# First memory's keys with high and low parts side by side: a wide and a narrow product per row chunk, one half copied by ScalarE and the other added by VectorE

## The chip, the cores and the metric

The kernel runs on one core of a Trainium2 chip. The metric is the device time of one launch in microseconds (us); lower is better. Engine names are those of the profile: PE is TensorE (PEld its weight loads), DVE is VectorE, ACT is ScalarE, POOL is GpSimd, SP issues the transfers. Each engine runs its own list of instructions in order, and semaphores tie the lists together.

## What is computed

Two transformer blocks over 256 tokens of width 1024, all in float32. The first block is a gated feed-forward, a mix of two attentions (eight latent heads, "mla", and four differential heads, "diff"), a second feed-forward and a gated embedding. The second block has two layers, each with a mixer, an attention over a memory of 256 rows, and a feed-forward. What the change touches are the memory's keys in the first of these layers:

```python
def memory_cross_attention(x, mem_n, w_q, w_k, w_v, w_o):
    q = (x @ w_q).reshape(B, S, XA_HEADS, XA_DH)
    k = (mem_n @ w_k).reshape(B, -1, XA_HEADS, XA_DH)
    v = (mem_n @ w_v).reshape(B, -1, XA_HEADS, XA_DH)
    s = jnp.einsum('bshd,bmhd->bhsm', q, k).astype(jnp.float32) * (XA_DH ** -0.5)
    p = jax.nn.softmax(s, axis=-1).astype(x.dtype)
```

`mem_n @ w_k` depends on inputs alone, so the kernel computes it long before it is used, between the steps of the first block's attentions.

## The kernel before

**Split numbers.** The large products run in a replicated float32 format whose inputs are cut short, so every operand is kept as a high part and a low part (the rest). A product is three: high by high, high by low, low by high, summed in one bank of PSUM (`three`, L1966 to L1972). A weight block is 128 x 1024 numbers. SP fetches it into one of four raw buffers, ACT writes its high part (`w_hi`, L617), DVE its low part (`w_lo`, L1158), and PE uses it. ACT and DVE work four blocks ahead of PE: each engine's `blk()` stands for "PE has come to this block", and starts the conversion of the block four places on.

**The memory.** Its normalised rows, turned so that features lie on partitions, are held as `m_hi` and `m_lo` (each 128 x 8 x 256). For layer 0 there are 16 memory blocks (`mem_blocks(0, ...)`): first eight for the values, then eight for the keys, called key 0 to key 7 here. A key block is one `chunk` of 8 row chunks: for each, three products with 128 x 128 weights and 256 moving columns, all into the first half of a bank. The banks are 6 and 7 in turn (`k_bank`). ACT then copies the 256 columns to `k_mem` (L804) and adds one to the semaphore `mem_evac`. PE starts key n only when the bank's last user has been copied out:

```python
def k_evacs(l, k):
    if l == 0:
        return 4 + (0 if k < 2 else k if k == 6 else k - 2 if k == 7 else k - 1)
```

So keys 2, 3, 4 and 5 wait for `mem_evac` of 5, 6, 7 and 8: four copies of values, and the keys up to n - 2.

**The loop over twelve heads** (four diff, then eight mla) is where the keys stand. `KV_FILL = (0, 1, 2, 3, 4, 9, 11)` names the rounds with a key block: key 0 comes ahead of the loop, keys 1 to 5 in PE's rounds 0 to 4, key 6 in round 9, key 7 in round 11. In its round i the engines do, in this order:

- PE: the key block; the scores of head i + 1 (L2289 for diff, L2296 for mla); the turn of the probabilities of head i - 1 (L2313), which waits for DVE's last step on them; the weighted sum of head i - 2 (L2326, L2334).
- DVE: `softmax_in(i)` (bias and row maximum: L1512, L1515 for diff, L1518, L1519 for mla; for diff heads from 2 on it waits for the turn of head i - 2); `softmax_out(i - 1)` (division: L1527 to L1533 for diff, L1536, L1538 for mla); if i - 2 is a round with a key, `blk()`, that is a `w_lo` of four blocks on; then the low part of an mla head's output (L1176).
- ACT: the exponentials of head i (L819, L824); if i - 1 is a round with a key, its copy (L804) and a `w_hi`; the copy of turned probabilities (L830); the output copy of head i - 2.

The loop starts some 276 us into the run, and the output projection `w_out` follows it at 328.8 us.

Of the kernel before, what the change touches and what calls it, by code (L numbers as in the profile page):

```python
# [9 lines left out]
F32R = mybir.dt.float32r  # L10
I32 = mybir.dt.int32
ALU = mybir.AluOpType
ACT = mybir.ActivationFunctionType
# [3 lines left out]
P = 128  # L17
S = 256
D = 1024
DC = D // P  # L20
# [22 lines left out]
TILES = 8  # L43
# [125 lines left out]
def build(nc, x_d, xT_d, mem_d, pT, prm_d, id_d, cst_d, late_d, row_d, w_d, out):  # L169
    with ExitStack() as ctx:  # L170
        def sb(name, shape, dt=F32):
            return ctx.enter_context(nc.sbuf_tensor(name, shape, dt))
# [4 lines left out]
        PB = [ctx.enter_context(nc.psum_tensor(f"bank{i}", [P, 512], F32)) for i in range(8)]  # L177
# [8 lines left out]

        x_hi = sb("x_hi", [P, DC, S], F32R)
        x_lo = sb("x_lo", [P, DC, S], F32R)
        m_hi = sb("m_hi", [P, DC, S], F32R)
        m_lo = sb("m_lo", [P, DC, S], F32R)  # L190

        h_hi = sb("h_hi", [P, 8, S], F32R)
        h_lo = sb("h_lo", [P, 8, S], F32R)
# [21 lines left out]
        k_mem = [kv_mem[:, 2 * l, :].rearrange("p (c s) -> p c s", s=S) for l in range(2)]  # L215
# [4 lines left out]
        rs_tok = [tokst[:, 16 + 2 * v:18 + 2 * v] for v in range(4)]  # L220
# [23 lines left out]
        def flat(ap):  # L244
            return ap.rearrange("p a b -> p (a b)")
# [27 lines left out]
        dv, at = region(at, 2, 512)  # L273
# [80 lines left out]
        def sems(names):  # L354
            return [sem(n) for n in names.split()]
# [9 lines left out]
        hi_ready, lo_ready, block_done, vec_chain = sems("hi_ready lo_ready block_done vec_chain")  # L365
        res_ready, xh_ready, xl_ready, y_ready, na_ready, nd_ready, xn_ready, xd_ready, over_alpha = sems(
            "res_ready xh_ready xl_ready y_ready na_ready nd_ready xn_ready xd_ready over_alpha")
        proj_sq, var_ready, lat_norm, lat_t, lat_hi, lat_lo, v_up, vup_evac, dv_evac = sems(
            "proj_sq var_ready lat_norm lat_t lat_hi lat_lo v_up vup_evac dv_evac")
        dq_sum, dq_n, dq_t, diff_evac, dk_n, dk_t = sems(  # L370
            "dq_sum dq_n dq_t diff_evac dk_n dk_t")
        f_gu, k_n, kr_n, k_t, k_evac, q_rot, q_t, q_up = sems("f_gu k_n kr_n k_t k_evac q_rot q_t q_up")
        mem_stat, mem_xn, mem_t, mem_g, mem_hi, mem_lo, mem_evac = sems("mem_stat mem_xn mem_t mem_g mem_hi mem_lo mem_evac")
# [60 lines left out]
        KV_FILL = (0, 1, 2, 3, 4, 9, 11)  # L434
        KV_FREE = 16 - len(KV_FILL)
# [34 lines left out]
        def k_bank(l, k):  # L470
            return PB[(4 if l == 1 and k < 2 else 6) + (k + (l == 0 and k >= 6)) % 2]
# [135 lines left out]
        def _(act):  # L607
# [190 lines left out]
            def mem_blocks(l, lo, hi):  # L798
                for m in range(lo, hi):
                    b = nb[0]  # L800
                    kind, k, i = fill(l, m)
                    if kind == "k":
                        done(b)
                        nc.scalar.activation(k_mem[l][:, k, :], k_bank(l, k)[:, 0:S], ACT.Copy).then_inc(mem_evac, 1)  # L804
                    elif i == 3:
                        done(b)
                        for t in range(2):
                            nc.scalar.activation(v_mem[l][:, t, k * HALF:(k + 1) * HALF], v_bank(l, k)[t][:, :], ACT.Copy, scale=1.0 / ALPHA
                                                 ).then_inc(mem_evac, 1)
                    blk()  # L810
# [100 lines left out]
            for k, (a, n) in enumerate(LAT_PARTS):  # L911
                for t in range(2):
                    nc.scalar.activation(lat_n[:, t, a:a + n], PB[4 + t][:, a:a + n], ACT.Copy,
                                         scale=lat_r[:, 2 * k + t:2 * k + t + 1]).then_inc(lat_norm, 1)
# [27 lines left out]
                nc.scalar.activation(flat(dk[:, 2 * j:2 * j + 2, :]), PB[j][:, :], ACT.Copy, scale=col("g_diff_k")).then_inc(diff_evac, 1)  # L942
            done(blk())
            for t in range(2):
                nc.scalar.activation(dv[:, t, :], PB[2 + t][:, :], ACT.Copy, scale=rs_tok[1][:, t:t + 1]).then_inc(dv_evac, 1)
            mem_blocks(0, 0, 2)
            blk()
            done(blk())
# [63 lines left out]
            for n in range(20):  # L1012
                b = FIRST["ab_in"] + n
# [123 lines left out]
        def _(dve):  # L1137
# [28 lines left out]
            def blk():  # L1166
                behind(nb[0])
                nb[0] += 1
                return nb[0] - 1
# [327 lines left out]
            def mem_blocks(lo, hi):  # L1497
                for m in range(lo, hi):
                    blk()
# [115 lines left out]
            for k, (_, n) in enumerate(LAT_PARTS):  # L1615
                ins = of_raw(lat_ss[:, 2 * k:2 * k + 2], rv[:, 500 + 2 * k:502 + 2 * k], n)
# [69 lines left out]
            for t in range(2):  # L1686
                for g in range(2):
                    k = 2 * t + g
# [10 lines left out]
            settle()  # L1699
            link(nc.vector.tensor_tensor(qr, qr, of_heads(rope_cos[0]), ALU.mult))  # L1700
            nc.vector.tensor_tensor(qr, qr, q_sin, ALU.add).then_inc(q_rot, 1)
            mem_blocks(5, KV_FREE)

            for i in range(NH + 3):
                if i < NH:
                    softmax_in(i, HEADS[i])
                if 1 <= i < NH + 1:
                    softmax_out(i - 1, HEADS[i - 1])
                if i - 2 in KV_FILL:
                    blk()  # L1710
                if i >= 3:
                    head_lo(i - 3, HEADS[i - 3])
                if i == 8:
                    dve.wait_ge(do_stat, 1)
                    link(nc.vector.tensor_scalar(rv[:, 0:S], PB[6][:, 0:S], 1.0 / DIFF_V, RMS_EPS, ALU.mult, ALU.add))
                    rsqrt_guess(rows[:, 0:S], rv[:, 0:S])
                if i in (9, 10):
                    link(rsqrt_steps(rows[:, 0:S], rv[:, 0:S], 1))
                if i == 11:
                    rsqrt_steps(rows[:, 0:S], rv[:, 0:S], 1).then_inc(do_rows, 1)  # L1720
                if i == 12:
                    for h in range(DIFF_HEADS):
                        dve.wait_ge(do_bc, h // 2 + 1)
                        nc.vector.scalar_tensor_tensor(d_out[:, h, :], d_out[:, h, :], g_sub_scaled, half(1 - h // 2, h),
                                                       ALU.mult, ALU.mult).then_inc(do_n, 1)
                if i == 13:
                    for h in range(DIFF_HEADS):
                        dve.wait_ge(do_hi, h + 1)
                        low(x_lo[:, 4 + h, :], d_out[:, h, :], x_hi[:, 4 + h, :], do_lo)
# [120 lines left out]
            for h in range(HG_HEADS):  # L1850
# [6 lines left out]
                for n in range(1, NCHUNK - 1):  # L1857
                    settle()
                    ins = nc.vector.scalar_tensor_tensor(state_of(h, n + 1), state_of(h, n),
                                                         decay[:, h * NCHUNK + n:h * NCHUNK + n + 1],  # L1860
                                                         PB[n % 4][:, n // 4 * P:n // 4 * P + P], ALU.mult, ALU.add)
# [96 lines left out]
        def _(pe):  # L1958
# [6 lines left out]
            def arrived(b):  # L1965
                pe.wait_ge(lo_ready, split_of(b))  # L1966
# [7 lines left out]
            def tile(b, n, w=P):  # L1974
                s = slice(n * P, n * P + w)
                return w_hi[:, slot(b), s], w_lo[:, slot(b), s]

            def chunk(b, out, hi, lo, ready=None):

                arrived(b)  # L1980
                for k in range(TILES):
                    if ready:
                        ready(k)
                    ins = three(out, *tile(b, k), hi[:, k, :], lo[:, k, :], start=k == 0, stop=k == TILES - 1)
                ins.then_inc(block_done, 1)
# [153 lines left out]
            def token_ffn(f, b0):  # L2139
# [114 lines left out]
                                False, True, first=y_ready)  # L2254
                nb[0] = b1 + FFN_BLOCKS

            def mem_blocks(l, lo, hi):
                for m in range(lo, hi):
                    b = blk()
                    kind, n, i = fill(l, m)  # L2260
                    if kind == "k":
                        if l == 0 or n >= 2:
                            pe.wait_ge(mem_evac, k_evacs(l, n))
                        if l == 0 and n == 7:
                            pe.wait_ge(s_max, 10)
                        chunk(b, k_bank(l, n)[:, 0:S], m_hi, m_lo)
                        continue
                    if i == 0 and (l or n):
                        pe.wait_ge(mem_evac, 20 if l else 2)
                        if l and n:  # L2270
                            pe.wait_ge(na_ready, 2 * LN[8] + 2)
                            pe.wait_ge(nd_ready, 2 * LN[8] + 2)
                    arrived(b)
                    for k in range(2):
                        for t in range(2):
                            c, q, w = 2 * i + k, slice(t * P, (t + 1) * P), slice(k * HALF, (k + 1) * HALF)
                            ins = three(v_bank(l, n)[t][:, :], m_hi[:, c, q], m_lo[:, c, q], w_hi[:, slot(b), w], w_lo[:, slot(b), w],
                                        start=i == 0 and k == 0, stop=i == 3 and k == 1)
                    ins.then_inc(block_done, 1)
# [132 lines left out]
            for n, (kind, i) in enumerate(IN_ORDER):  # L2412
# [7 lines left out]
                if n == 9:  # L2420
                    pe.wait_ge(lat_norm, 6)
                    for c in range(3):
                        for t in range(2):
                            ins = nc.tensor.transpose(half(4 + c // 2, c)[:, t * P:(t + 1) * P], lat_n[:, t, c * P:(c + 1) * P], ident)
                    ins.then_inc(lat_t, 1)

            b = blk()
# [33 lines left out]
            pe.wait_ge(mem_lo, 4)  # L2461
            mem_blocks(0, 0, 2)

            pe.wait_ge(diff_evac, 4)
            pe.wait_ge(dv_evac, 2)
            for k in range(2):
                b = blk()
                arrived(b)
                for t in range(2):
                    s = slice(t * P, (t + 1) * P)  # L2470
                    for g in range(2):
                        o = slice(4 * QK * g, 4 * QK * (g + 1))
                        ins = three(PB[2 * t + g][:, 0:4 * QK], h_hi[:, k, s], h_lo[:, k, s], w_hi[:, slot(b), o], w_lo[:, slot(b), o],
                                    start=k == 0, stop=k == 1)
# [393 lines left out]
```

## Time and profile before

| what | value |
|---|---|
| time, median of 3 runs | 1265.15 us (1263.97 to 1265.7) |
| the profiled execution's own time | 1267.17 us |
| its span in the trace | 1265.3 us |
| PE busy, share of the span | 1254.2 us, 99% |
| DVE busy, share of the span | 826.5 us, 65% |
| ACT busy, share of the span | 660.9 us, 52% |
| mean granted TensorE clock | 0.997 of full speed |

A busy PE in the table means that some product was in flight. The start of each product is recorded, and the distance from one start to the next tells how fast PE works; the ends overlap. A timeline row gives the start in us, the duration in us (of all that the row merges), engine, line, operation, tiles written and read, shapes and how many; square brackets hold the idle time ahead and who ended it. A single float32 product is recorded as two, so "x4" is two products in those rows.

### The profile page before, as it was taken

To read this page: it belongs to the slowest core of one execution; us is meant where nothing else is said; L and a number is where in the kernel's file an instruction comes from. 1 tells how busy PE (TensorE), PEld (TensorE's weight loads), DVE (VectorE), ACT (ScalarE), POOL (GpSimd) and SP (SyncE) were. 2 spreads that over 40 slices of the span, in tenths; PEclk is the share of its full clock that TensorE was granted. 3 is DMA by queue.
4 is the path that set the end of the run, shared out by engine and by line. 5 is a ranking of instruction groups with operands and counts; after the bars stand their busy time and mean duration, and the time that the engine had idled before them with its cause. 6 is when DMAs were issued, how large, how long until landed. Compare 5 with 4: busy or idle time off the path is not lost.

```text
span 1265.3 us, 16736 instructions
## 1 busy us (share of the span) xinstructions
PE 1254.2 (99%) x6592; PEld 1077.2 (85%) x6592; DVE 826.5 (65%) x1268; ACT 660.9 (52%) x999; POOL 28.8 (2%) x33
## 2 busy tenths in 40 slices
PE   9999999999999999999999999999999999999998
PEld 8888888888888888899999897888888998888886
DVE  6655666878767565667998665755557575755554
ACT  7544546667574444454526655644445654644443
POOL 0000000010000000000000000000001000000000
PEclk9999999999999999999998999999999999999999
DMA  9655555542355555554424543755555442655552
GB/s 348 216 184 183 185 184 195 170 165 84 126 179 187 184 187 194 184 168 150 150 96 140 199 134 116 249 186 184 198 183 167 167 150 85 228 187 193 189 184 65
DMA packets 62572, 218.94 MB, mean 173 GB/s; under 512 B 6688, under 2 KB 10016, under 8 KB 61984
## 3 DMA queue, kind: packets, MB, share of 16 engines
q1 hardware_dynamic: 62352, 217.63, 51.1%
q8 instruction: 52, 0.85, 0.3%
q10 hardware_dynamic: 144, 0.26, 0.1%
q14 instruction: 24, 0.20, 0.0%
HBM read 216.81 MB, written 1.05 MB: 172 GB/s over the span
## 4 chain that ended last, share of the span: by engine, by line
PE 91%; DVE 7%; ACT 1%; issue 0%; DMA 0%; POOL 0%; DVEq 0%; ACTq 0%; POOLq 0%
PE bank L1970 27%; PE bank L1972 26%; PE bank L1971 26%; DVE arena L1794 3%; PE bank L2194 2%; DVE w_lo L1158 1%; PE bank L2341 1%; PE bank L2302 1%; PE bank L1992 1%; PE bank L2313 1%; PE bank L2405 1%; PE bank L2091 0%; PE bank L2058 0%; PE bank L2296 0%; PE bank L2631 0%
## 5 line engine op out<-in xcount | busy, mean ns | idle before, releaser
L1158 DVE TENSOR_TENSOR w_lo<-w_raw,w_hi 128x1024 fp32r<-128x1024 f32 x382 | 466.3, 1225 | 332.2 <-ACT w_hi L617 330.4
L617 ACT ACTIVATE w_hi<-w_raw 128x1024 fp32r<-128x1024 f32 x382 | 403.3, 1059 | 446.6 <-PE bank L1972 427.7
L1970 PE MATMUL bank<-w_hi,x_hi 128*128 128x512 f32 (+2 forms) x912 | 353.8, 388 | 0.4 <-DVE x_lo L1180 0.4
L1972 PE MATMUL bank<-w_hi,x_lo 128*128 128x512 f32 (+2 forms) x912 | 349.6, 383 | 0.0
L1971 PE MATMUL bank<-w_lo,x_hi 128*128 128x512 f32 (+2 forms) x912 | 349.4, 383 | 0.0
L1972 PEld LDWEIGHTS bank<-w_hi,x_lo 128*128 128x128 f32 x912 | 171.4, 188 | 33.2
L1970 PEld LDWEIGHTS bank<-w_hi,x_hi 128*128 128x128 f32 x912 | 171.5, 188 | 32.7 <-DVE x_lo L1180 0.7
L1971 PEld LDWEIGHTS bank<-w_lo,x_hi 128*128 128x128 f32 x912 | 171.5, 188 | 32.1
L1970 PE MATMUL bank<-w_hi,h_hi 128*128 128x512 f32 (+1 forms) x364 | 142.4, 391 | 0.0
L1972 PE MATMUL bank<-w_hi,h_lo 128*128 128x512 f32 (+1 forms) x364 | 141.3, 388 | 0.0
L1971 PE MATMUL bank<-w_lo,h_hi 128*128 128x512 f32 (+1 forms) x364 | 141.2, 388 | 0.0
L1970 PEld LDWEIGHTS bank<-w_hi,h_hi 128*128 128x128 f32 x364 | 68.3, 188 | 14.7 <-DVE h_lo L1176 1.1
L1972 PEld LDWEIGHTS bank<-w_hi,h_lo 128*128 128x128 f32 x364 | 68.3, 188 | 14.0
L1971 PEld LDWEIGHTS bank<-w_lo,h_hi 128*128 128x128 f32 x364 | 68.4, 188 | 13.5
L1970 PE MATMUL bank<-x_hi,w_hi 128*128 128x256 f32 x256 | 74.3, 290 | 1.5 <-DVE arena L1817 0.9
L1971 PE MATMUL bank<-x_lo,w_hi 128*128 128x256 f32 x256 | 72.4, 283 | 0.0
L1972 PE MATMUL bank<-x_hi,w_lo 128*128 128x256 f32 x256 | 72.4, 283 | 0.0
L1970 PEld LDWEIGHTS bank<-x_hi,w_hi 128*128 128x128 f32 x256 | 49.1, 192 | 2.2 <-DVE arena L1817 1.1
L1794 DVE SCALAR_TENSOR_TENSOR arena<-arena,prm 128x256 f32<-128x256 f32 x120 | 50.0, 478 | 0.5
L1971 PEld LDWEIGHTS bank<-x_lo,w_hi 128*128 128x128 f32 x256 | 49.1, 192 | 0.2
L1972 PEld LDWEIGHTS bank<-x_hi,w_lo 128*128 128x128 f32 x256 | 49.1, 192 | 0.0
L1992 PE MATMUL bank<-xs,w_raw 128*128 128x256 f32 x192 | 43.0, 381 | 0.2 <-DVE xs L1758 0.2
(323 smaller groups left out, 1379.2 us busy)
## 6 DMA issues: line engine op xcount, KB each, us to landing
w_raw<-weights_d SPq DMA_DIRECT2D x394, 512.0 KB, 3.3
arena<-weights_d SPq DMA_DIRECT2D x4, 512.0 KB, 5.7
arena<-ln_rows_d SPq DMA_DIRECT2D x2, 1024.0 KB, 5.6
arena<-late_d SPq DMA_DIRECT2D x1, 1056.0 KB, 5.6
xs<-x_d SPq DMA_DIRECT2D x2, 512.0 KB, 7.4
kv_mem<-mem_d SPq DMA_DIRECT2D x1, 1024.0 KB, 9.4
out_d<-xs SPq DMA_DIRECT2D x4, 256.0 KB, 2.3
arena<-xT_d SPq DMA_DIRECT2D x3, 256.0 KB, 6.2
```

What stands on the lines that cost most here:

```text
L617: nc.scalar.activation(w_hi[:, slot(b), :], w_raw[:, b % RAW, :], ACT.Copy).then_inc(hi_ready, 1)
L1158: nc.vector.tensor_tensor(w_lo[:, slot(b), :], w_raw[:, b % RAW, :], w_hi[:, slot(b), :].bitcast(F32), ALU.subtract).then_inc(lo_ready, 1)
L1794: ins = nc.vector.scalar_tensor_tensor(conv[:, c, :], src, w, conv[:, c, :], ALU.mult, ALU.add)
L1970: nc.tensor.matmul(out, wh, xh, start=start, stop=False, skip_group_check=True)
L1971: nc.tensor.matmul(out, wh, xl, start=False, stop=False, skip_group_check=True)
L1972: return nc.tensor.matmul(out, wl, xh, start=False, stop=stop, skip_group_check=True)
L1992: ins = nc.tensor.matmul(out, w_raw[:, b % RAW, k * P:(k + 1) * P], x[:, k, 0, :], start=k == 0, stop=k == TILES - 1)
L2194: ins = nc.tensor.transpose(PB[2 + k][:, at:at + P], hf[:, t, (2 * k + j) * P:(2 * k + j + 1) * P], ident)
L2302: ins = nc.tensor.matmul(half(n % 2, t), xq[:, 2 * h + k, t * P:(t + 1) * P], k_mem[l][:, 2 * h + k, :], start=k == 0, stop=k == 1)
L2313: ins = nc.tensor.transpose(PB[2 + n % 2][:, k * S + t * P:k * S + (t + 1) * P], e_buf(n)[:, 0, t, k * P:(k + 1) * P], ident)
L2341: ins = nc.tensor.matmul(o[:, c * S:(c + 1) * S], v_mem[l][:, k, at:at + P], pt_buf(n)[:, k, :], start=c == 0 and k == 0, stop=k == 1, ski ...
L2405: nc.tensor.matmul(out, ones, ones, start=True, stop=True)
```

## The change

`m_hi` and `m_lo` become two halves of one buffer `m_hl` (128 x 8 x 2 x 256), so that a row chunk's high and low parts lie side by side. For layer 0's keys, a new `key_chunk` takes the place of `chunk`: with the weights' high part, one product over 512 columns (high and low) into a whole bank; with their low part, one product over 256 columns (high) into the bank's first half. ACT copies the second half to `k_mem` and adds one to a new semaphore `key_side`. DVE waits for that, adds the first half (`key_sum`), and now DVE's add gives `mem_evac`. `key_sum(0)` stands ahead of DVE's loop, the others in the rounds with a `blk()`, behind `softmax_out` and ahead of `blk()`. Layer 1's keys are as before. The semaphore `dv_evac` is merged into `diff_evac`.

```diff
-        m_hi = sb("m_hi", [P, DC, S], F32R)
-        m_lo = sb("m_lo", [P, DC, S], F32R)
+        m_hl = sb("m_hl", [P, DC, 2, S], F32R)
+        m_hi, m_lo = m_hl[:, :, 0, :], m_hl[:, :, 1, :]
...
-                    if kind == "k":
+                    if kind == "k" and l == 0:
+                        done(b)
+                        nc.scalar.activation(k_mem[l][:, k, :], k_bank(l, k)[:, S:2 * S], ACT.Copy).then_inc(key_side, 1)
+                    elif kind == "k":
...
+            def key_sum(k):
+
+                dve.wait_ge(key_side, k + 1)
+                keys = k_mem[0][:, k, :]
+                nc.vector.tensor_tensor(keys, k_bank(0, k)[:, 0:S], keys, ALU.add).then_inc(mem_evac, 1)
+
             mem_blocks(5, KV_FREE)
+            key_sum(0)
...
                 if 1 <= i < NH + 1:
                     softmax_out(i - 1, HEADS[i - 1])
                 if i - 2 in KV_FILL:
+                    key_sum(KV_FREE - DC + KV_FILL.index(i - 2))
                     blk()
...
+            def key_chunk(b, bank):
+
+                arrived(b)
+                for k in range(TILES):
+                    wh, wl = tile(b, k)
+                    nc.tensor.matmul(bank[:, :], wh, flat(m_hl[:, k, :, :]), start=k == 0, stop=k == TILES - 1, skip_group_check=True)
+                    ins = nc.tensor.matmul(bank[:, 0:S], wl, m_hl[:, k, 0, :], start=False, stop=k == TILES - 1, skip_group_check=True)
+                ins.then_inc(block_done, 1)
...
-                        chunk(b, k_bank(l, n)[:, 0:S], m_hi, m_lo)
+                        if l:
+                            chunk(b, k_bank(l, n)[:, 0:S], m_hi, m_lo)
+                        else:
+                            key_chunk(b, k_bank(l, n))
...
-            pe.wait_ge(diff_evac, 4)
-            pe.wait_ge(dv_evac, 2)
+            pe.wait_ge(diff_evac, 6)
```

DVE's list in the kernel before, from the end of round 2 (`softmax_out(1)`, then the `w_lo`) into round 3:

```order
L1530 TENSOR_SCALAR kv_mem<-kv_mem,small 128x256 x2
L1533 SCALAR_TENSOR_TENSOR kv_mem<-kv_mem,small 128x256 [waits vec_chain]
L1533 SCALAR_TENSOR_TENSOR kv_mem<-kv_mem,small 128x256
L1158 TENSOR_TENSOR w_lo<-w_raw,w_hi 128x1024 [waits hi_ready]
L1512 ISA kv_mem,small<-bank,arena 128x256 [waits t_ps,bias_in,s_ps]
```

The same place in the changed kernel (the file's lines have moved by three):

```order
L1533 TENSOR_SCALAR kv_mem<-kv_mem,small 128x256 x2
L1536 SCALAR_TENSOR_TENSOR kv_mem<-kv_mem,small 128x256 [waits vec_chain]
L1536 SCALAR_TENSOR_TENSOR kv_mem<-kv_mem,small 128x256
L1709 TENSOR_TENSOR kv_mem<-bank,kv_mem 128x256 [waits key_side]
L1161 TENSOR_TENSOR w_lo<-w_raw,w_hi 128x1024 [waits hi_ready]
L1515 ISA kv_mem,small<-bank,arena 128x256 [waits t_ps,bias_in,s_ps]
```

The add of key 1 stands between the last step on head 1's probabilities and the `w_lo`, and is the second add to give `mem_evac`.

PE's list in the kernel before, from the scores of head 2 (end of round 1) into key 3 (round 2):

```order
L2289 MATMUL bank<-arena 128x256 [waits s_biased]
L2289 MATMUL bank<-arena 128x256 x3
L2313 MATMUL bank<-ident,kv_mem 128x128 [waits s_prob,q_up]
L2313 MATMUL bank<-ident,kv_mem 128x128 x3
L1970 MATMUL bank<-m_hi,w_hi 128x256 [waits lo_ready,mem_evac]
L1971 MATMUL bank<-m_lo,w_hi 128x256
L1972 MATMUL bank<-m_hi,w_lo 128x256
L1970 MATMUL bank<-m_hi,w_hi 128x256
```

The same place in the changed kernel:

```order
L2312 MATMUL bank<-arena 128x256 [waits s_biased]
L2312 MATMUL bank<-arena 128x256 x3
L2336 MATMUL bank<-ident,kv_mem 128x128 [waits s_prob,q_up]
L2336 MATMUL bank<-ident,kv_mem 128x128 x3
L2273 MATMUL bank<-m_hl,w_hi 128x512 [waits lo_ready,mem_evac]
L2274 MATMUL bank<-m_hl,w_lo 128x256
L2273 MATMUL bank<-m_hl,w_hi 128x512
```

Nothing changes place on PE: three rows of a row chunk are now two, and the key block's first product waits for the same count of `mem_evac`, which another engine now gives.

## Rows read from the trace of the kernel before

**Rows 1.** The page: the chain that ended last, share of the span by engine.

```profile
PE 91%; DVE 7%; ACT 1%; issue 0%; DMA 0%; POOL 0%; DVEq 0%; ACTq 0%; POOLq 0%
```

**Rows 2.** Timeline, PE: 512-column products of a value block, 256-column products of key 0.

```profile
267.87 0.39 PE L1970 MATMUL bank<-w_hi,m_hi 128*128 128x512 f32 x1
...
268.55 0.39 PE L1970 MATMUL bank<-w_hi,m_hi 128*128 128x512 f32 x1
...
273.38 0.28 PE L1970 MATMUL bank<-m_hi,w_hi 128*128 128x256 f32 x1
...
275.54 0.28 PE L1970 MATMUL bank<-m_hi,w_hi 128*128 128x256 f32 x1
```

**Rows 3.** Timeline, PE, rounds 1 to 3: turns, scores, first products of keys 3 and 4.

```profile
285.34 0.66 PE L2313 MATMUL bank<-ident,kv_mem 128*128 128x128 f32 x4
285.75 0.36 PE L1970 MATMUL bank<-m_hi,w_hi 128*128 128x256 f32 x1
...
288.79 1.14 PE L2289 MATMUL bank<-arena 64*128 64x256 f32 x8
289.87 0.66 PE L2313 MATMUL bank<-ident,kv_mem 128*128 128x128 f32 x4
291.04 0.47 PE L1970 MATMUL bank<-m_hi,w_hi 128*128 128x256 f32 x1
...
294.10 1.03 PE L2296 MATMUL bank<-arena 96*128 96x256 f32 x4
```

**Rows 4.** Timeline, PE: key 5, the scores of head 5, the turn of head 5.

```profile
296.08 0.47 PE L1970 MATMUL bank<-m_hi,w_hi 128*128 128x256 f32 x1
...
299.14 1.03 PE L2296 MATMUL bank<-arena 96*128 96x256 f32 x4
...
304.52 0.66 PE L2313 MATMUL bank<-ident,kv_mem 128*128 128x128 f32 x4
```

**Rows 5.** Timeline, DVE, rounds 2 to 5: one row at each point where a step begins.

```profile
286.17 0.42 DVE L1512 CUSTOM_DVE_ANT_0 kv_mem<-bank,rlat 128x256 f32<-128x256 f32 x1 [1.40 <-PE bank L2313]
...
289.54 1.22 DVE L1158 TENSOR_TENSOR w_lo<-w_raw,w_hi 128x1024 fp32r<-128x1024 f32 x1
290.70 0.42 DVE L1512 CUSTOM_DVE_ANT_0 kv_mem<-bank,arena 128x256 f32<-128x256 f32 x1
...
294.06 1.22 DVE L1158 TENSOR_TENSOR w_lo<-w_raw,w_hi 128x1024 fp32r<-128x1024 f32 x1
295.20 0.68 DVE L1518 TENSOR_REDUCE small<-bank 128x2 f32<-128x512 f32 x1
...
297.77 1.22 DVE L1158 TENSOR_TENSOR w_lo<-w_raw,w_hi 128x1024 fp32r<-128x1024 f32 x1
300.20 0.69 DVE L1518 TENSOR_REDUCE small<-bank 128x2 f32<-128x512 f32 x1 [1.21 <-PE bank L2296]
...
303.86 0.61 DVE L1538 TENSOR_SCALAR kv_mem<-kv_mem,small 128x256 f32<-128x256 f32 x2
```

**Rows 6.** Timeline, ACT: the copy of key 1.

```profile
285.02 0.36 ACT L804 ACTIVATE kv_mem<-bank 128x256 f32<-128x256 f32 x1
```

**Rows 7.** Timeline, DVE: a 128 x 256 step that reads a bank.

```profile
310.50 0.42 DVE L1715 TENSOR_SCALAR rv<-bank 128x256 f32<-128x256 f32 x1 [0.89 <-PE bank L2347]
```

**Rows 8.** Timeline, PE: the turn of head 11.

```profile
325.06 0.66 PE L2313 MATMUL bank<-ident,kv_mem 128*128 128x128 f32 x4 [1.04 <-DVE kv_mem L1538]
```

**Rows 9.** Busy us by stretch (PE, PEld, DVE, ACT, POOL), then granted clock, DMA.

```profile
670.00:675.00 5.00, 5.00 (x28) 5.00 (x28) 3.91 (x6) 0.66 (x2) 1.53 (x1) 0.57 0.32 104
675.00:680.00 5.00, 5.00 (x35) 5.00 (x34) 4.86 (x16) 2.56 (x7) 0.84 (x2) 0.75 0.33 109
```

**Rows 10.** Timeline, PE, around that stretch.

```profile
669.80 2.76 PE L2637 MATMUL bank<-ones,arena 128*128 128x1 f32 x16
...
675.45 0.41 PE L1970 MATMUL bank<-m_hi,w_hi 128*128 128x256 f32 x1
675.66 0.41 PE L1971 MATMUL bank<-m_lo,w_hi 128*128 128x256 f32 x1
```

More of the change, by code:

```diff
@@ L367, in build @@
             "res_ready xh_ready xl_ready y_ready na_ready nd_ready xn_ready xd_ready over_alpha")
-        proj_sq, var_ready, lat_norm, lat_t, lat_hi, lat_lo, v_up, vup_evac, dv_evac = sems(
-            "proj_sq var_ready lat_norm lat_t lat_hi lat_lo v_up vup_evac dv_evac")
+        proj_sq, var_ready, lat_norm, lat_t, lat_hi, lat_lo, v_up, vup_evac, key_side = sems(
+            "proj_sq var_ready lat_norm lat_t lat_hi lat_lo v_up vup_evac key_side")
         dq_sum, dq_n, dq_t, diff_evac, dk_n, dk_t = sems(
@@ L944, in _ @@
             for t in range(2):
-                nc.scalar.activation(dv[:, t, :], PB[2 + t][:, :], ACT.Copy, scale=rs_tok[1][:, t:t + 1]).then_inc(dv_evac, 1)
+                nc.scalar.activation(dv[:, t, :], PB[2 + t][:, :], ACT.Copy, scale=rs_tok[1][:, t:t + 1]).then_inc(diff_evac, 1)
             mem_blocks(0, 0, 2)
```

## The prediction

> **What bounds the kernel now.** I read the page's chain first: it is PE for 91% of the span [rows 1], and PE is busy 99% of it. What shortens PE's stream shortens the run, and what makes PE wait lengthens it by as much, unless a wait stood there already. The second view is PE's timeline at the two widths that matter. A 512-column product starts every 0.227 us (0.68 over three), a 256-column one every 0.120 us (2.16 over eighteen) [rows 2]: 0.2135 per 512 columns, and some 0.0135 that each product costs beside its columns. The third is the loop over the heads, engine by engine. PE's keys fill the time in which DVE does the softmax: key 3 starts at 285.75, and when it and the scores behind it are through, the turn of head 1 starts at 289.87 [rows 3], 0.3 us after DVE has finished head 1's probabilities at about 289.6 (the `w_lo` behind them starts at 289.54) [rows 5]. So key 3 covers exactly the time that DVE needs. I asked of each key what it waits for now and what it waits for then.
>
> **The products: a small gain.** Before, a row chunk is 3 x 0.120 = 0.360 us; after, 0.227 + 0.120 = 0.347. A block of eight row chunks gets 0.104 shorter, eight blocks 0.83 us. The columns are the same 768; only one product's fixed cost in three goes. The weight loads go from three to two as well, but they run beside the products.
>
> The Trainium skill ("TensorE: Matmul & The Clock Gate", section "Back-to-back issue gap") gives the fixed part of a warm product as about 2.5 ns; by that figure the 64 products saved would be an estimated 0.16 us. The rows show 13 ns at both widths, and the trace decides.
>
> **ScalarE's side** costs nothing: it copies 256 columns per key as before (0.36 us [rows 6]), from the other half of the bank. The high and low parts' new places change no count of instructions, and the merged semaphore waits for the same copies.
>
> **The adds.** DVE gets eight of them, 128 x 256, one input from a bank. The nearest row is a step of that size that reads a bank, 0.42 us [rows 7]. That would be 3.4 us on an engine that is 65% busy. Their place matters more than their length, because the copy that lets PE go on is now the last of three steps on DVE.
>
> **Key 3, the wait that the change adds.** Key 3 waits for `mem_evac` of 6, that is for key 1 to be out of bank 7. Before, ACT's copy of key 1 ends at 285.02 + 0.36 = 285.38 [rows 6], ahead of key 3's start at 285.75: PE did not wait. After, the count comes from `key_sum(1)`, which DVE's list holds in round 2 behind `softmax_in(2)` and `softmax_out(1)`. DVE starts the first at 286.17 and is through the second at 289.54 [rows 5]; the add takes 0.42 and the hand-over to PE 0.05 (the turn at 304.52 against a DVE step that ends at 303.86 + 0.61 = 304.47 [rows 4, 5]). That is 290.0. The add of key 0 ahead of the loop puts off round 0 by up to 0.42, of which PE's earlier end of keys 0 to 2 takes some back; I take 0.2. Key 3 starts at 290.2 where it started at 285.75: **+4.4 us**. Queued behind it on PE are the scores of head 3 and the turn of head 1, and behind these scores stands DVE's next round. Key 3 no longer covers the softmax; it follows it, and the next softmax follows key 3.
>
> **Key 4.** It waits for the add of key 2, in DVE's round 3. From key 3's start: key 3 to the scores behind it 288.79 - 285.75 - 0.10 = 2.94; scores to turn 1.08 [rows 3]; from the turn's start to `softmax_in` 286.17 - 285.34 = 0.83 [rows 3, 5] (a diff head's waits for that turn); `softmax_in(3)` and `softmax_out(2)` 294.06 - 290.70 = 3.36 [rows 5]; add and hand-over 0.47. Sum 8.68, so key 4 starts at 298.9, against 291.04 before [rows 3]: **+7.8 us**.
>
> **Key 5.** It waits for the add of key 3, in DVE's round 4. Key 4 to the scores of head 4: 294.10 - 291.04 - 0.10 = 2.96 [rows 3]; scores to `softmax_in` of an mla head 300.20 - 299.14 = 1.06 [rows 4, 5]; `softmax_in(4)` and `softmax_out(3)` 297.77 - 295.20 = 2.57 [rows 5]; 0.47. Sum 7.06, so 305.9 against 296.08 [rows 4]: **+9.8 us**. That is the end of this chain: key 6 comes in round 9 and key 7 in round 11, and the adds that they wait for are rounds back by then.
>
> **The rest of the loop.** The scores of head 5 follow key 5 at +9.7. The adds of keys 4 and 5 lie in DVE's rounds 5 and 6, where DVE releases PE without slack: the turn of head 5 starts 0.05 after its DVE step [rows 4, 5]. Of their 0.84 I take 0.7. Keys 6 and 7 give back 0.2. The add of key 6 lies in DVE's round 11, in which PE already waits 1.04 us for DVE at 325.06 [rows 8]: +0.4. The add of key 7 falls between other waits and costs between 0 and 0.4; I take 0, since the first two weight blocks' products of the output projection cover the low parts that come behind it. Together 9.7 + 0.7 - 0.2 + 0.4 = **+10.6 us**. After the loop PE is the bound again and nothing gives back a delay that all engines share.
>
> **The clock.** PE is quiet from the end of the turn of head 0 (about 286.0) to 290.2, then from about 295.7 to 298.9 and from about 304.2 to 305.9. The trace has one place where the granted clock fell. It was 0.57 in 670 to 675 and 0.75 in 675 to 680 [rows 9]; with 0.5 (1.2 of 2.4 GHz) as the lower level that is 4.3 + 2.5 = 6.8 us at half. Ahead of it PE had only one-column products and a few transposes [rows 10]. A 256-column product then started every 0.21 us [rows 10]. Such a fall costs at most half of its 6.8 us, 3.4, and less where part of it passes in a quiet stretch. Key 3's block all at half would take 2.8 us more by doubling; the pitch says 0.09 us per 256 columns, 8 x 3 x 0.093 = 2.2. So I take 2.3 for a fall in the quiet ahead of key 3, and 1.2 for the second quiet, three quarters as long, as about even odds of another: **+3.5 us**, with 0 and 10.2 (three full falls) as ends.
>
> The Trainium skill (same page, section "What's actually happening") says that a quiet TensorE is throttled to half its clock and comes back after sustained work; the fall in the trace agrees. What that adds is in the 3.5.
>
> **Sum.** The profiled execution has a span of 1265.3 in a time of 1267.17, and the median is 1265.15; I add the difference to the median. 10.6 + 3.5 = 14.1, which gives **1279.3 us**.
>
> **The rivals.**
>
> *The clock holds.* The chain of waits is as worked out, but no quiet stretch brings a fall: 1265.15 + 10.6 = 1275.8. For it: the quiets are a few us long, with dense products between. Against it: the trace's fall came with PE working, if sparsely.
>
> *The clock falls in every round.* Three falls near the full 3.4: 1275.8 + 10.2 = 1286. It needs each fall to lie wholly in work, while the quiets take a part of each.
>
> *The adds come in time (not slower).* DVE is idle for 1.40 us up to 286.17 [rows 5], and key 1's copy is out at 285.38 [rows 6]; an add in that gap would end near 285.8, and key 3 would not wait. It decides at key 3's old start, 285.75: if the count of 6 is there by then, the keys stay covers, only the 0.83 is left, and the time is 1264.3; with the adds of rounds 5, 6 and 11 charged, 1265.4. Against it: DVE's list holds the add behind `softmax_out(1)`, and engines do not change places in their lists.
>
> *Only part of the chain forms.* If DVE's rounds shrink since they no longer share anything with PE, or keys 4 and 5 find their counts sooner than summed, the delay is key 3's 4.4 and a part of the rest: 1270 to 1273.
>
> **How the numbers follow.** The forecast, chain and one or two falls, gets 0.62; the clock that holds 0.18; falls in every round 0.09; part of the chain 0.06; adds in time 0.05. The range leaves out the last two and the far end of the third: 1274.8 (the clock holds, less 1.0 for the small terms) to 1285. A measurement of this kernel can tell about 0.2%, 2.5 us, from no change. Faster by that much would need 2.5 us where the products give 0.83: 0.01. Within it: 0.05. Slower: 0.94.
>
> **What would show it.** In the profile after: 512-column products of the keys every 0.227 us and narrow ones every 0.120; idle time of some 4 us on PE (or its weight loads) ahead of key 3, 3 ahead of key 4 and 1.7 ahead of key 5, released by DVE's add; key starts near 290.2, 298.9 and 305.9 with a full clock, later by 2 to 3 with a fall; an add of 0.42; the granted clock below 1 between 286 and 312 and nowhere new; the output projection some 14 us later than at 328.8. Wrong would be: no wait of PE on the add; ACT's copy as the last step; a wide product that takes more than two narrow ones; or a delay of the loop that does not show in the end.

## Result, and the profile after

| | before | after |
|---|---|---|
| median | 1265.34 us (4 runs) | 1280.08 us (1278.79 to 1280.41, 4 runs) |
| span of the profiled execution | 1265.3 us | 1278.0 us |
| PE busy | 1254.2 us | 1256.0 us |
| DVE busy | 826.5 us | 829.2 us |
| ACT busy | 660.9 us | 660.5 us |
| mean granted clock | 0.997 | 0.995 |

The changed kernel is slower: the ratio is 1.0111, with a 95% interval of 1.0099 to 1.0123, some 14.7 us. The forecast was 1279.3. One execution of the first variant below, the one with narrow products, took 3036.11 us and is left out of its ratio. The engines' busy times have hardly moved. What has moved is when they work. The waits of PE in the loop over the heads (engine, line, who it waited for: total us, times, longest), in the changed kernel:

```profile
PE bank L2273 <- DVE kv_mem L1709: 8.9, 3, 4.0
PE bank L2336 <- DVE kv_mem L1541: 2.2, 3, 1.5
PE bank L2312 <- DVE small L1515: 0.3, 1, 0.3
```

L2273 is the wide product, L1709 DVE's add: three waits, 8.9 us, which the kernel before does not have. Where they stand, in PE's timeline (start, duration; first product of keys 3, 4 and 5, and what PE does around them):

```profile
286.84 0.66 PE L2336 MATMUL bank<-ident,kv_mem 128*128 128x128 f32 x4
291.51 0.80 PE L2273 MATMUL bank<-m_hl,w_hi 128*128 128x512 f32 x1 [4.01 <-DVE kv_mem L1709]
...
296.64 1.14 PE L2312 MATMUL bank<-arena 64*128 64x256 f32 x8
297.72 0.66 PE L2336 MATMUL bank<-ident,kv_mem 128*128 128x128 f32 x4
298.21 1.03 PE L2349 MATMUL bank<-kv_mem,arena 128*128 128x256 f32 x4
302.38 0.50 PE L2273 MATMUL bank<-m_hl,w_hi 128*128 128x512 f32 x1 [3.15 <-DVE kv_mem L1709]
...
310.95 0.50 PE L2273 MATMUL bank<-m_hl,w_hi 128*128 128x512 f32 x1 [1.79 <-DVE kv_mem L1709]
```

In [rows 3] key 3 starts 0.4 us after the start of the turn ahead of it; here it is 4.7 us. DVE's side of the first wait, and what the wait then does to DVE:

```profile
287.68 0.42 DVE L1515 CUSTOM_DVE_ANT_0 kv_mem<-bank,rlat 128x256 f32<-128x256 f32 x1 [1.34 <-PE bank L2336]
...
291.04 0.42 DVE L1709 TENSOR_TENSOR kv_mem<-bank,kv_mem 128x256 f32<-128x256 f32 x1
291.37 1.22 DVE L1161 TENSOR_TENSOR w_lo<-w_raw,w_hi 128x1024 fp32r<-128x1024 f32 x1
298.55 0.42 DVE L1515 CUSTOM_DVE_ANT_0 kv_mem<-bank,arena 128x256 f32<-128x256 f32 x1 [5.96 <-PE bank L2336]
```

The add ends at 291.46 and PE starts at 291.51. After its `w_lo` DVE is idle for 5.96 us, for PE. In [rows 5] the two softmax rounds follow each other at 286.17 and 290.70, with no idle time. PE waits for DVE, then DVE for PE: what ran side by side now takes turns.

The granted clock (the column after the five engines' busy times), by stretch:

```profile
285.00:290.00 5.00, 2.50 (x18) 1.60 (x16) 3.55 (x17) 3.98 (x14) 0.00 (x0) 0.94 0.01 2
290.00:295.00 5.00, 3.49 (x11) 3.02 (x12) 2.55 (x5) 2.67 (x8) 0.00 (x0) 0.50 0.28 86
295.00:300.00 5.00, 4.24 (x23) 2.98 (x21) 1.45 (x8) 1.25 (x3) 0.00 (x0) 0.87 0.05 19
300.00:305.00 5.00, 2.62 (x10) 2.25 (x11) 3.36 (x11) 3.29 (x10) 0.00 (x0) 0.81 0.11 24
305.00:310.00 5.00, 4.16 (x20) 3.31 (x18) 2.01 (x7) 1.40 (x4) 0.00 (x0) 0.85 0.21 81
```

With 0.5 as the lower level (1.2 of 2.4 GHz), the missing parts are (0.06 + 0.50 + 0.13) x 10 = 6.9 us for the first fall and (0.19 + 0.15) x 10 = 3.4 us for the second. While the clock is at half, the wide products of key 3 start every 0.64 us:

```profile
292.31 0.63 PE L2273 MATMUL bank<-m_hl,w_hi 128*128 128x512 f32 x1
292.75 0.41 PE L2274 MATMUL bank<-m_hl,w_lo 128*128 128x256 f32 x1
292.96 0.63 PE L2273 MATMUL bank<-m_hl,w_hi 128*128 128x512 f32 x1
```

At full clock, in key 0 and key 5, a row chunk takes 0.35.

To set runs side by side I use distances from key 0's first product, since its start differs by up to 1.3 us between executions (272.94 to 274.24):

| us from key 0's start to | key 3 | key 4 | key 5 | key 6 | key 7 | output projection |
|---|---|---|---|---|---|---|
| before | 12.81 | 18.10 | 23.14 | 39.34 | 46.54 | 55.88 |
| after | 17.27 | 28.14 | 36.71 | 53.42 | 60.53 | 70.19 |
| difference | +4.46 | +10.04 | +13.57 | +14.08 | +13.99 | +14.31 |

The loop alone has grown by 14.3 us. The spans differ by 12.7 only; the last experiments show why.

### The profile page after: what moved, and what is told of

Read it like the earlier page. It is cut to its first block, busy times and chain, and to the rows that moved or that the text cites. A ratio compares the mean times of both kernels' runs of the same rounds, so it can differ in the third digit from the quotient of the medians.

```text
span 1278.0 us, 16616 instructions
## 1 busy us (share of the span) xinstructions
PE 1256.0 (98%) x6528; PEld 1073.6 (84%) x6528; DVE 829.2 (65%) x1276; ACT 660.5 (52%) x999; POOL 28.9 (2%) x33
## 4 chain that ended last, share of the span: by engine, by line
PE 87%; DVE 9%; DMA 1%; ACT 1%; issue 1%; SPq 0%; POOL 0%; DVEq 0%; ACTq 0%; POOLq 0%
PE bank L1981 26%; PE bank L1983 25%; PE bank L1982 25%; DVE arena L1805 3%; DVE w_lo L1161 2%; PE bank L2205 2%; DMA w_raw<-weights_d 1%; PE bank L2273 1%; PE bank L2364 1%; PE bank L2325 1%; PE bank L2003 1%; PE bank L2274 1%; PE bank L2336 1%; ACT w_hi L617 0%; PE bank L2069 0%
## 5 line engine op out<-in xcount | busy, mean ns | idle before, releaser
L1981 PEld LDWEIGHTS bank<-w_hi,h_hi 128*128 128x128 f32 x364 | 68.3, 188 | 14.7 <-DVE h_lo L1179 1.1
```

Source lines behind the costliest of these rows:

```text
L1981: nc.tensor.matmul(out, wh, xh, start=start, stop=False, skip_group_check=True)
```

## Experiments

Three theories stood against each other. **The wait**: an add behind `softmax_out` in DVE's list makes the key blocks follow the softmax, and the loss is what stands ahead of the add; the clock falls in the quiets that this makes. **The work**: the eight adds cost as work on DVE, wherever they stand. **The product**: the wide product or the new layout is slow.

### The product: three narrow products, all else as changed

```diff
-                    nc.tensor.matmul(bank[:, :], wh, flat(m_hl[:, k, :, :]), ...)
+                    nc.tensor.matmul(bank[:, 0:S], wh, m_hl[:, k, 0, :], ...)
+                    nc.tensor.matmul(bank[:, S:2 * S], wh, m_hl[:, k, 1, :], ...)
```

> The changed kernel with three narrow products per row chunk (the high by low one into the bank's second half), and the same copy, add and waits. The theory of the wait: the products are a small matter, so nearly the whole 14.7 us stay, and the time is the changed kernel's 1280.1 plus up to 0.8, 1280 to 1281.5; key 3 still starts some 4 us after the turn. The rival, that the wide product or the new layout is what costs: back to 1265 to 1268.

Measured: 1279.28 us against 1266.81 for the kernel before in the same job, ratio 1.0095 (1.0077 to 1.0114). That is 12.5 us more, and the time lies below the expected 1280 to 1281.5; no run looks for the cause, but the fall of the clock behind the loop, with which this section ends, is of about this size. The loop does show the expected size: key 0 to the output projection takes 70.63 us, 14.75 more than before and 0.44 more than with the wide product. PE's waits for the add are the same:

```profile
PE bank L2273 <- DVE kv_mem L1709: 8.9, 3, 4.0
PE bank L2337 <- DVE kv_mem L1541: 2.1, 3, 1.4
```

So the product theory falls: with the old products the loss stays. By the loop of the two traces the wide product is a gain, and a small one; the run times cannot tell it.

### The place of the add: at the head of DVE's round

```diff
             for i in range(NH + 3):
+                if i - 2 in KV_FILL:
+                    key_sum(KV_FREE - DC + KV_FILL.index(i - 2))
                 if i < NH:
...
                 if i - 2 in KV_FILL:
-                    key_sum(KV_FREE - DC + KV_FILL.index(i - 2))
                     blk()
```

> The changed kernel with each add moved to the head of DVE's round, ahead of softmax_in, into the idle time that DVE has there. The theory of the wait: key 3 starts within 0.3 us of the turn before it, the granted clock stays full in the loop, and the time is 1264.3 to 1266.5 (the adds of rounds 3 to 6 may still push the softmax by 0.4 each). The rival, that the eight adds cost as work on DVE wherever they stand: 1268 or more.

Measured: 1267.22 us against 1266.81 us for the kernel before in the same job, ratio 1.0005 (0.9996 to 1.0014): no difference that can be told. The forecast was given on a base of 1265.3; as a difference from the kernel before it was -1.0 to +1.2, and 0.4 was measured. DVE's first add in the loop, and key 3 on PE:

```profile
286.24 0.42 DVE L1709 TENSOR_TENSOR kv_mem<-bank,kv_mem 128x256 f32<-128x256 f32 x1 [0.64 <-ACT kv_mem L804]
286.95 0.42 DVE L1515 CUSTOM_DVE_ANT_0 kv_mem<-bank,rlat 128x256 f32<-128x256 f32 x1 [0.29 <-PE bank L2337]
```

```profile
286.12 0.66 PE L2337 MATMUL bank<-ident,kv_mem 128*128 128x128 f32 x4
286.72 0.50 PE L2274 MATMUL bank<-m_hl,w_hi 128*128 128x512 f32 x1
```

The add fits into idle time that DVE had, and the 8.9 us of waits are gone. Key 3 starts 0.60 us after the turn, where 0.3 was expected and the kernel before has 0.41. The same adds, the same products, the same copies: the place of one line in DVE's list is worth all of the loop's 14.3 us but 1.25. Key 0 to the output projection takes 57.13 us, 1.25 more than before, although the eight key blocks are shorter. A part of that stands ahead of key 2, where PE waits for the row maximum of round 0, and DVE now has the add of key 0 ahead of it:

```profile
280.96 1.14 PE L2313 MATMUL bank<-arena 64*128 64x256 f32 x8 [0.34 <-DVE small L1515]
```

### The place again: between the two halves of the softmax

```diff
                     softmax_in(i, HEADS[i])
+                if i - 2 in KV_FILL:
+                    key_sum(KV_FREE - DC + KV_FILL.index(i - 2))
                 if 1 <= i < NH + 1:
                     softmax_out(i - 1, HEADS[i - 1])
                 if i - 2 in KV_FILL:
-                    key_sum(KV_FREE - DC + KV_FILL.index(i - 2))
                     blk()
```

> The changed kernel with each add between softmax_in and softmax_out of its round. The theory of the wait, by the same rows: key 3 +2.6, key 4 +4.2, key 5 +4.4 and the loop +5.3 against the kernel before; the quiets are 2.2 and 1.5 us, so no fall or one of 2: ratio 1.004 to 1.0055, that is 5 to 7 us. The rival, a loss that does not grow with what stands ahead of the add on VectorE: as at the head of the round (same as before) or as behind softmax_out (14 us).

Measured: 1273.54 us against 1266.17, ratio 1.0060 (1.0047 to 1.0073), 7.4 us. PE's waits are at keys 3 and 4, and key 5 finds its count:

```profile
289.16 0.50 PE L2274 MATMUL bank<-m_hl,w_hi 128*128 128x512 f32 x1 [2.23 <-DVE kv_mem L1709]
297.67 0.50 PE L2274 MATMUL bank<-m_hl,w_hi 128*128 128x512 f32 x1 [1.36 <-DVE kv_mem L1709]
```

```profile
290.00:295.00 5.00, 5.00 (x24) 3.87 (x23) 2.02 (x3) 2.12 (x6) 0.00 (x0) 0.66 0.32 105
```

Key 3 is at 15.50 us from key 0, +2.7 against the kernel before (expected 2.6). The granted clock of 0.66 in one stretch is 3.4 us at half. Key 3's products take 4.35 us from the first start to the last, where the run with filler below, at full clock, has 2.81, so the fall costs 1.5. The loop takes 62.73 us, +6.85, and less 1.5 that is +5.3, as expected. The time is a little above the expected 5 to 7 us; the interval (6.0 to 9.2) reaches into it. The loss grows with what DVE has ahead of the add, as the theory of the wait says and the two others do not.

### The wait alone: old products, no adds

The kernel before, with `mem_evac` given by a one-column step on DVE in the place of the add:

```diff
-                        nc.scalar.activation(k_mem[l][:, k, :], k_bank(l, k)[:, 0:S], ACT.Copy).then_inc(mem_evac, 1)
+                        nc.scalar.activation(k_mem[l][:, k, :], k_bank(l, k)[:, 0:S], ACT.Copy).then_inc(mem_evac if l else key_side, 1)
...
+                dve.wait_ge(key_side, k + 1)
+                nc.vector.tensor_copy(small[:, 52:53], neg_lam).then_inc(mem_evac, 1)
```

> The kernel before (three narrow products, one half bank, ScalarE's copy), but mem_evac now comes from a one-column step of VectorE that waits for ScalarE's copy and stands where the changed kernel has its add. The wait without the add and without the new products. The theory of the wait: key 3 +4.0, key 4 +7.2, key 5 +9.1 against the kernel before, the loop +9.4, and with the clock's falls of the changed kernel (+3.7, the quiets are as long) 13 us more than before, ratio 1.0103. The rival, that the adds as work made the loss: under 3 us.

Measured: 1277.56 us against 1266.17, ratio 1.0090 (1.0077 to 1.0103), 11.4 us.

```profile
PE bank L1977 <- DVE small L1705: 8.1, 3, 3.7
```

```profile
290.00 0.15 DVE L1705 COPY small<-small 128x1 f32<-128x1 f32 x1
```

A step of 0.15 us that computes nothing of use makes three waits, 8.1 us in all. Key 3 is at 16.82, +4.0 as expected; the loop takes 67.94 us, +12.1 where 13.1 was expected. The theory of the work falls as an account of the loss. The estimate was 1 us too high because of the clock. I had put its falls at the changed kernel's 3.7 us, and here both are short, 3.4 us at half each:

```profile
290.00:295.00 5.00, 4.80 (x26) 4.58 (x28) 1.27 (x3) 1.63 (x4) 0.00 (x0) 0.66 0.32 105
300.00:305.00 5.00, 4.83 (x26) 4.74 (x27) 1.25 (x3) 1.61 (x4) 0.00 (x0) 0.66 0.31 105
```

Against the kernel before, key 3's products take 1.3 us more, key 4's 1.0, and the scores behind key 4 some 0.3. That is 2.7 for the clock, and 9.4 is left for the chain of waits, as expected. From key 5 on this kernel loses 0.1 us and the changed one 0.7; this kernel has no adds there, so I put that part down to them.

### The clock: products of ones in the quiets

PE computes 17, 13 and 6 extra products of ones ahead of keys 3, 4 and 5; the results are not used.

```diff
                 if i in KV_FILL:
+                    if i in (2, 3, 4):
+                        pe.wait_ge(k_evac, 4)
+                        if i == 4:
+                            pe.wait_ge(do_sq, 1)
+                        warm(half(4 if i == 4 else 5, 1)[:, 0:P], (17, 13, 6)[i - 2])
```

> The changed kernel with 17, 13 and 6 extra products of ones (128 columns, results unused) on PE ahead of keys 3, 4 and 5, in the quiets. The theory of the clock: with PE at work the clock stays full, key 4 starts some 8.7 and key 5 some 15.7 us after key 3, and the time is 3 to 4 us below the changed kernel's, 1276 to 1277. The rival, that the key blocks are slow for another reason (the layout, bank traffic): they stay at 0.64 us per row chunk and the time stays at 1280.

Measured: 1275.94 us, ratio 1.0075 (1.0061 to 1.0088); the run with narrow products, on the same chip in the same job, is at 1279.28. The expected time was 1276 to 1277, 3 to 4 us below the changed kernel's.

```profile
286.07 3.96 PE L2428 MATMUL bank<-ones 128*128 128x128 f32 x34
290.25 0.50 PE L2273 MATMUL bank<-m_hl,w_hi 128*128 128x512 f32 x1 [0.21 <-DVE kv_mem L1709]
...
299.01 0.50 PE L2273 MATMUL bank<-m_hl,w_hi 128*128 128x512 f32 x1 [0.24 <-DVE kv_mem L1709]
...
306.06 0.50 PE L2273 MATMUL bank<-m_hl,w_hi 128*128 128x512 f32 x1 [0.46 <-DVE kv_mem L1709]
```

```profile
290.00:295.00 5.00, 4.79 (x30) 3.82 (x30) 1.32 (x2) 1.41 (x4) 0.00 (x0) 1.00 0.32 105
300.00:305.00 5.00, 5.00 (x33) 4.46 (x33) 1.98 (x8) 1.46 (x5) 0.00 (x0) 1.00 0.33 108
```

The clock stays at 1.00 throughout the loop. Key 4 follows key 3 after 8.76 us, key 5 after another 7.05, the whole loop takes 66.58: +10.7 against the kernel before. This is the chain of waits by itself, and 70.19 - 66.58 = 3.6 us is what the two falls cost. They cost it in the products of two keys: key 3's take 4.93 us in the changed kernel and 2.81 here, key 4's 4.33 and 2.81, so 2.1 us for the first fall and 1.5 for the second. The waits that the list shows have almost gone (0.9 us in all), since filler stands in them: a busy PE is not a useful one.

### The bank freed by ScalarE, and who adds

ScalarE copies both halves and gives `mem_evac`; DVE adds from SBUF in the old place, and PE waits for the adds only at the output projection:

```diff
-                        nc.scalar.activation(k_mem[l][:, k, :], k_bank(l, k)[:, S:2 * S], ACT.Copy).then_inc(key_side, 1)
+                        nc.scalar.activation(k_mem[l][:, k, :], k_bank(l, k)[:, S:2 * S], ACT.Copy)
+                        if k >= 3:
+                            act.wait_ge(key_side, k - 2)
+                        nc.scalar.activation(k_high[:, k % 3, :], k_bank(l, k)[:, 0:S], ACT.Copy).then_inc(mem_evac, 1)
...
-                nc.vector.tensor_tensor(keys, k_bank(0, k)[:, 0:S], keys, ALU.add).then_inc(mem_evac, 1)
+                nc.vector.tensor_tensor(keys, k_high[:, k % 3, :], keys, ALU.add).then_inc(key_side, 1)
```

> The changed kernel, but ScalarE copies both halves of the bank (the high one to a buffer of its own in SBUF, of three places) and its second copy gives mem_evac; DVE adds from SBUF where it did, and PE waits for the adds only before the output projection's second half. The theory of the wait: PE no longer follows DVE's list, and the time is 1265 to 1268, with ScalarE's eight more copies of 0.36 us partly on the path in rounds 5 to 7. The rival, that the adds cost as work: 1268 or more with the place of the add on DVE unchanged.

Measured: 1266.93 us against 1266.81, ratio 1.0000 (0.9992 to 1.0009). The loop takes 57.04 us, +1.2, with the adds where the changed kernel has them. Part of what is left of the loss shows in PE's small waits in rounds 5 to 7, for DVE and for ScalarE:

```profile
305.76 0.66 PE L2340 MATMUL bank<-ident,kv_mem 128*128 128x128 f32 x4 [0.36 <-DVE kv_mem L1545]
307.47 1.13 PE L2323 MATMUL bank<-arena 96*128 96x256 f32 x4 [0.18 <-ACT kv_mem L831]
308.75 0.66 PE L2340 MATMUL bank<-ident,kv_mem 128*128 128x128 f32 x4 [0.15 <-DVE kv_mem L1545]
```

Then the same with the adds on GpSimd:

```diff
             distances(3)
+            for k in range(DC):
+                pool.wait_ge(mem_evac, 4 + k + 1)
+                keys = k_mem[0][:, k, :]
+                nc.gpsimd.tensor_tensor(keys, k_high[:, k % 3, :], keys, ALU.add).then_inc(key_side, 1)
```

> As the run in which ScalarE copies both halves to SBUF, but GpSimd makes the eight adds (SBUF to SBUF), so that neither VectorE nor TensorE waits for them. If VectorE's adds are what ate the products' 0.8 us: the loop is 0.3 to 1 us shorter than with VectorE's adds, and the time 0.5 us below the kernel before. The rival, that GpSimd's access to SBUF slows VectorE, or that ScalarE's second copies are what costs: the loop is as long as or longer than with VectorE's adds, 1 us or more above the kernel before.

Measured: 1267.00 us against 1266.17, ratio 1.0006 (0.9996 to 1.0015). The loop takes 56.06 us, 1.0 less than with DVE's adds (expected 0.3 to 1), but still 0.2 more than before, so the half microsecond below the kernel before did not come. What takes the products' gain was not taken apart: ScalarE's second copies are left, and one group of DVE's steps (the division of mla heads, SBUF to SBUF) has a mean of 373 ns beside GpSimd's adds and 350 without. The first fence is that group (busy us, mean ns, idle us before); the second GpSimd's timeline, where an add takes 0.73 to 1.02 us, with time to spare:

```profile
L1549 DVE TENSOR_SCALAR kv_mem<-kv_mem,small 128x256 f32<-128x256 f32 x16 | 5.3, 373 | 0.3
```

```profile
276.89 0.73 POOL L591 TENSOR_TENSOR kv_mem<-k_high,kv_mem 128x256 f32<-128x256 f32 x1 [4.30 <-ACT k_high L812]
286.04 0.73 POOL L591 TENSOR_TENSOR kv_mem<-k_high,kv_mem 128x256 f32<-128x256 f32 x1 [8.41 <-ACT k_high L812]
```

None of the variants is measurably faster than the kernel before. A whole gain of 0.8 us would be 0.06% of the time, below what these measurements tell.

### The kernel before once more

> The kernel before, unchanged, for a second trace of it. The first has the clock at half for 6.8 us from 670; the traces of the changed kernel and of four variants, whose code is the same there, do not. If the fall comes with the place in the free-running clock's time and not with the code, this trace has it or not by chance; without it the span is 3 us shorter than the first trace's 1265.3, other things equal, and key 0 to the output projection takes 55.9 us as in the first.

Measured: 1266.33 us, span 1264.5 us; key 0 to the output projection takes 55.88 us, to the hundredth what the first trace has. The clock between 670 and 680:

```profile
670.00:680.00 10.00, 10.00 (x75) 10.00 (x75) 9.60 (x23) 3.92 (x9) 2.37 (x2) 0.83 0.33 107
```

That is 3.4 us at half where the first trace has 6.8 [rows 9], and the traces of the changed kernel and of the runs with narrow products, with the add at the head, with filler and with ScalarE's two copies (DVE's adds) have no fall there. The other three have one: 3.4 us with the add between the halves and with the wait alone, 6.8 with GpSimd's adds. From the output projection to the end the first trace takes 1265.3 - 328.8 = 936.5 us, this one 934.9, the changed kernel's 1278.0 - 344.4 = 933.6. The other traces line up with these: 934.7 and 934.9 with a fall of 3.4, 936.3 with one of 6.8, 933.3 to 934.1 with none. So a fall of 6.8 us costs about 3 us and one of 3.4 about 1.4, and the difference of the two profiled spans comes out: 14.3 in the loop, 1.3 ahead of it, less 2.9 behind it, is 12.7. I had expected a span 3 us shorter without any fall; this trace has half a fall, and its start lies 0.8 later. The code there is the same in both traces of this kernel, so the length of the fall differs from one execution to another; what decides it was not tried.

## Why the prediction was right

- **The products.** Forecast 0.10 us per key block, 0.83 in all. The blocks of keys 0, 5 and 6 are 0.06, 0.12 and 0.09 shorter; all eight together, with keys 3 and 4 from the run with filler, 0.68. Against three narrow products in the same setting the loop gains 0.44. That is 7 to 11 ns for each of the 64 products saved, where 13 were taken. Right in kind, between half and four fifths in size. The row chunks start every 0.347 us in some keys, which is the sum's figure, and every 0.353 in others. Why they differ is open.
- **The adds.** 0.42 us, as taken from the nearest row [rows 7].
- **Key 3** +4.4: +4.46, and the wait of 4.01 us names the add.
- **Keys 4 and 5** at full clock +7.8 and +9.8: with the filler they are at 26.04 and 33.09 from key 0, +7.9 and +9.95. The steps of key 4's sum (2.94, 1.08, 0.83, 3.36, 0.47) are 3.02, 1.07, 0.83, 3.36 and 0.48 there. The first is longer because key 3's block got only 0.02 shorter, not 0.10.
- **The rest of the loop**, +10.6 in all: +10.7 with the filler.
- **The clock**, forecast 3.5 us, measured 3.6. I took 2.3 for the first fall; 4.7 us of its 6.8 lay in work (291.5 to 296.2), and it cost 2.1. The second was taken as even odds of another one of the same price, 1.2. It came, but half as long: 3.4 us, wholly in work, for 1.5. That the sum came out to 0.1 us is luck: a fall that had been charged at half its price came with half its length. The run with the wait alone, whose two falls cost 2.7, shows how far it can be off with nearly the same quiets. The Trainium skill ("TensorE: Matmul & The Clock Gate", section "What's actually happening") says that TensorE is throttled when quiet; here the trace agrees, with 0.50 granted in 290 to 295, and the filler run shows the other side, 1.00. The fall at 670 in the trace before, which I had also taken as agreeing, came with PE busy throughout, if with one-column products and a few transposes [rows 9, 10]; so a quiet is not the only thing that goes with a fall.
- **The rival of adds in time** decides where the forecast said it would, by the place in DVE's list: with the add at the head, and nothing else changed, the loss is gone but for 1.25 us in the loop. Its price was too low by 1 us: I had 0.83 gained and the adds of rounds 5, 6 and 11 charged, 1265.4, which is +0.25. The adds of rounds 5 and 6 cost 0.7 (key 6 against key 5) and that of round 11 0.3, as charged. But at key 5 the loop stands at +0.3, where five shorter blocks would give -0.5 by the sum; the wait of 0.34 us ahead of key 2 is a part of that, the rest was not taken apart.
- **Behind the loop** I said that nothing gives a delay back. For the median this holds within its interval: the loop's 14.3 stands against 14.7 (12.5 to 15.6). For one trace against another it does not, since the clock's fall at 670 comes and goes.

## What to carry to other kernels

A semaphore says when, but the list of the engine that gives it says after what. When the step that frees a buffer moves to another engine, go through that engine's list ahead of it up to the last point where it waited for the engine that now waits. All of that becomes the price, less what the waiting engine still has to do meanwhile. It is paid in each round where the two depend on each other so, and here it could be read from the old trace to 0.2 us. And if a block of work is there to cover another engine's step, a dependence on the end of that step undoes the cover: look for such filler before giving it a new input. Then add the clock: here quiets of 4.0, 3.1 and 2.2 us were followed by falls that cost 2.1, 1.5 and 1.5 us.

## What the hardware showed

- A row chunk of one 512-column and one 256-column product takes 0.347 to 0.353 us at full clock and 0.64 at half, three products of 256 columns 0.36. The columns are the same; one product and one weight load fewer give 7 to 13 ns.
- Every fall of the clock between a run's first and last microseconds, in ten traces, lasted 3.4 or 6.8 us. In the loop they came with PE quiets of 4.0 and 3.1 us, and with one of 2.2; quiets of 1.8 and 1.4 us had none. With filler of 128-column products in the quiets none came. The falls between 670 and 690, in five of the ten traces, came with no wait of PE longer than 0.2 us between 660 and 690.
- GpSimd adds 128 x 256 numbers from SBUF in 0.73 to 1.02 us beside a busy DVE. Of DVE's larger steps in the loop only the SBUF to SBUF scaling of the mla heads got slower, 373 ns against 350; the same scaling of the diff heads stayed at 350, the weights' `w_lo` at 1220.
